# Where the memory steps of a mixing phase stand among its attention heads, the order of its first loads, and four banks for a state update

## What is computed

```python
def step(carry, blk):                       # the matrix memory, branch A
    s = einsum('bhtd,bhsd->bhts', qb, kb) * dmat
    num = einsum('bhts,bhsv->bhtv', s, vb) + w_inter[..., None] * einsum('bhvd,bhtd->bhtv', C, qb)
    h = num / maximum(abs(den), exp(-m_t))[..., None]
    C_new = w_prev[..., None, None] * C + einsum('bhs,bhsv,bhsd->bhvd', w_s, vb, kb)

def sparse_attend(q, k_sel, v_sel, valid):  # branch B
    s = where(valid, einsum('btngd,btknd->btngk', q, k_sel) * B_HD ** -0.5, -inf)
    return einsum('btngk,btknd->btngd', softmax(s), v_sel)

y = sigmoid(a_o) * h * silu(a_z)                       # A, then a projection
merged = sigmoid(g_a) * (ya @ w_a_proj) + sigmoid(g_b) * (yb @ w_b_proj)
x = x + rmsnorm(merged @ w_out, norm_post)             # then a gated layer embedding
```

## Time and profile before

| | us |
|---|---|
| median of 3 runs | 3930.36 (3926.3 to 3934.82) |
| the profiled execution | 3925.36 |
| its span, first to last instruction | 3923.8 |
| mean granted TensorE clock | 0.979 |

### The profile page before, as it was taken

How to read it: one execution, slowest core, us unless ns; L and a number is a source line. 1 busy time by engine, 2 the same in 40 slices (tenths; PEclk the granted TensorE clock), 3 DMA queues, 4 the chain that set the end, 5 groups by cost and what they waited for, 6 DMA issues and landing times. The chain is left out here.

```text
span 3923.8 us, 56232 instructions
## 1 busy us (share of the span) xinstructions
PE 3757.7 (96%) x21590; PEld 2318.8 (59%) x21590; DVE 3012.1 (77%) x4178; ACT 1389.0 (35%) x2337; POOL 1667.8 (43%) x1529
## 2 busy tenths in 40 slices
PE   7899999999999999999999889989997999999999
PEld 4555555564456666666666466766664788854444
DVE  5589999879999999999999477677774677643333
ACT  5411211156244334433332356675552222111111
POOL 0000035549796566665555212234204666642121
PEclk9999999999999999999999899999997999999999
DMA  6312223240112111111211623464244665532111
GB/s 226 93 62 66 69 72 94 102 151 27 57 52 73 66 65 65 58 68 64 71 63 59 149 70 107 124 176 133 86 125 152 186 172 166 172 120 70 40 54 47
DMA packets 303453, 379.99 MB, mean 97 GB/s; under 512 B 74795, under 2 KB 227267, under 8 KB 299990
## 3 DMA queue, kind: packets, MB, share of 16 engines
q1 hardware_dynamic: 262790, 260.48, 22.0%
q0 software_dynamic: 19664, 86.31, 6.1%
q10 hardware_dynamic: 20736, 29.66, 2.4%
HBM read 245.79 MB, written 129.28 MB: 96 GB/s over the span
## 5 line engine op out<-in xcount | busy, mean ns | idle before, releaser
L1315 DVE MAX8 best<-score 128x8 f32<-128x384 f32 (+13 forms) x448 | 639.7, 1428 | 23.3 <-POOL score L1283 8.4
L1317 DVE MATCH_REPLACE8 score<-best,score 128x384 f32<-128x384 f32 (+13 forms) x448 | 631.1, 1409 | 0.0
L1072 PE MATMUL pr<-xnT,w_row 128*128 128x347 f32 (+1 forms) x960 | 298.7, 458 | 0.0
L1813 PE MATMUL mix_slot<-mix_kT,early 128*128 128x512 f32 (+3 forms) x640 | 271.2, 555 | 25.3 <-DMA mix_kT<-qt_scr 10.9
L1826 PE MATMUL mix_po<-mix_ring,mix_v 32*128 32x128 f32 x8704 | 264.9, 275 | 25.2 <-issue 13.3
L1224 POOL TENSOR_TENSOR kT<-kT 128x347 f32<-128x347 f32 (+1 forms) x240 | 193.7, 807 | 211.9 <-ACT kT L1142 204.9
L396 PE MATMUL pg<-xnT,wt 128*128 128x416 f32 x800 | 282.4, 516 | 0.0
L1826 PEld LDWEIGHTS mix_po<-mix_ring,mix_v 32*128 32x128 f32 x8704 | 255.3, 190 | 39.3 <-issue 30.1
L1072 PEld LDWEIGHTS pr<-xnT,w_row 128*128 128x128 f32 x960 | 180.6, 190 | 106.7 <-issue 11.6
L1142 ACT COPY kT<-pr 128x347 f32<-128x347 f32 (+1 forms) x240 | 106.5, 445 | 352.4 <-PE pr L1072 342.2
L396 PEld LDWEIGHTS pg<-xnT,wt 128*128 128x128 f32 x800 | 152.9, 191 | 127.9 <-issue 127.9
(11 more groups left out here) (626 smaller groups left out, 7848.3 us busy)
## 6 DMA issues: line engine op xcount, KB each, us to landing
gt_scr<-kT SPq DMA_DIRECT2D x40, 694.0 KB, 3.3
out_gm<-gt_scr ACTq DMA_DIRECT2D x32, 520.0 KB
gt_scr<-kT SPq DMA_DIRECT2D x20, 692.0 KB, 4.2
wt<-in_w_in SPq DMA_DIRECT2D x22, 512.0 KB, 4.0
w0a<-in_w_in SPq DMA_DIRECT2D x11, 1024.0 KB, 6.6
w_row<-in_w_in SPq DMA_DIRECT2D x10, 1024.0 KB, 6.7
qt_scr<-kT POOLq DMA_DIRECT2D x8, 1040.0 KB, 4.3
early<-ybt_scr SPq DMA_DIRECT2D x4, 2080.0 KB, 9.7
```

Of the source, the lines that this page charges most:

```text
L1072: ins = nc.tensor.matmul(pr[:, b, 0:w], lhs, rhs, start=k == 0, stop=k == 3)
L1315: nc.vector.max(best[:, :], sc).then_inc(top_step, 1)
L1317: nc.vector.match_replace(sc, best[:, :], sc, TAKEN).then_inc(top_step, 1)
L1813: mm(s[:, 0:width], bq[p][:, hh, :], kT[:, lo:lo + width], start=True, stop=True).then_inc(slot_mm, 1)
```

## The change

1. `memory_steps`: the 120 steps of tiles 1 to 15 stand only in the 88 heads with five key tiles or more, spread evenly, so that 32 of those heads take two. Heads 48 to 79 take none. The loads F go two a head.
2. `mixing_events`: X of unit 0 stands ahead of head 6's scores.
3. SP's first loads: the masks of unit 1 ahead of its queries, keys 3 behind them, the decays of tile 1 (L1612) ahead of tile 1's operands and of all values.
4. POOL's first three gathers (six indirect DMAs) stand at head 5, not at the start.
5. Sample memory: all 16 updates stand behind the last turn and take the four banks of `pc` in turn, so update u waits for u - 4; ACT decays the second half too (16 instructions more), and DVE's two products go; `spread_keys` stands behind the last `copy_tile`; POOL takes the weights' differences before the gates.

```diff
@@ def memory_steps
-    for m in range(1, NB):
-        for x, step in enumerate(tile(m)):
-            at[8 * m - 4 + x] = step
+    wide = [n for n in range(4, 8 * NB - 4) if MIX_UNITS[n // GQ][1] >= 4]
+    steps = [(m, x) for m in range(1, NB) for x in range(8)]
+    head = {step: wide[k * len(wide) // len(steps)] for k, step in enumerate(steps)}
+    for m, x in steps:
+        at[head[m, x]] = at.get(head[m, x], []) + tile(m)[x]
     for m in range(2, NB):
+        begin = head[m - 2, 6] + 1 if m > 2 else 4
         for x in range(7):
-            at[8 * m - 12 + x] = at.get(8 * m - 12 + x, []) + [("F", m, x)]
+            at[begin + x // 2] = at.get(begin + x // 2, []) + [("F", m, x)]
@@ def mixing_events
+            if u == 1 and h == 2:
+                events.extend(("X", x) for x in range(GQ))
+                turned = 1
@@ sample memory, POOL: ahead of pool.wait_ge(yb_loaded, 16)
+            pool.wait_ge(wb_loaded, 16 * (KT // 2))
+            for pair in range(COLUMN_PAIRS):
+                lo = 2 * P * pair
+                nc.gpsimd.tensor_tensor(w1[:, 0:4, lo + P:lo + 2 * P], w1[:, 0:4, lo:lo + P], w1[:, 0:4, lo + P:lo + 2 * P], ALU.subtract
+                                        ).then_inc(first_sums, 1)
@@ sample memory, DVE
                 dve.wait_ge(upd_mm, u + 1)
-                if half == 0:
-                    dve.wait_ge(decayed, 4 * (hh + 1))
-                nc.vector.tensor_tensor(C[:, bs, hh, x, :], C[:, bs, hh, x, :], pu[u % 2][:, :].rearrange("p (b e) -> p b e", b=4),
+                dve.wait_ge(decayed, 4 * AH * half + 4 * (hh + 1))
+                nc.vector.tensor_tensor(C[:, bs, hh, x, :], C[:, bs, hh, x, :], pc[:, hh // 2, hh % 2, :].rearrange("p (b e) -> p b e", b=4),
@@ sample memory, ACT
             copy_tile(5, 0)
+            copy_tile(6, 0)
             decay(2)
-            copy_tile(6, 0)
-            decay(3)
             copy_tile(7, 0)
             for x in range(QUARTERS):
                 gate(x)
+            decay(3)
+            act.wait_ge(c_turned, 2 * DB)
+            for hh in range(AH):
+                decay(hh, 1)
@@ sample memory, PE
-                if u < 2:
-                    pe.wait_ge(v.sem, v["qnr"])
-                else:
-                    pe.wait_ge(upd_done, u - 1)
+                if u == 0:
+                    wait_copied(DB - 2)
+                    wait_copied(DB - 1)
+                if u % 8 == 0:
+                    pe.wait_ge(v.sem, v[f"kwz{half}"])
+                if u >= 4:
+                    pe.wait_ge(upd_done, u - 3)
             for b in range(5, DB):
-                update(2 * b - 10)
                 turn(b)
-                update(2 * b - 9)
                 carried(b - 1)
-            update(6)
             carried(DB - 1)
-            for u in range(7, 16):
+            for u in range(16):
                 update(u)
```

More of the change, by code:

```diff
@@ L1679, in _ @@
             load_mask(0)
-            for g in range(1, KEY_GROUPS):
+            for g in (1, 2):
                 load_keys(0, g)
             load_first_values(0)
+            load_mask(1)
             load_queries(1)
-            load_mask(1)
+            load_keys(0, 3)
+            load_decay(sp, 1)
             load_first_memory(1)
@@ L1687, in _ @@
                 load_values(0, g)
-            load_decay(sp, 1)
             load_first_values(1)
@@ L1769, in _ @@
                 nc.gpsimd.memset(pw[x][:, :, :], 0.0).then_inc(s_zero, 1)
-            for j in range(KS - 1):
-                gather(j)
             for e in events:
                 i = e[1]
+                if e == ("S", GQ + 1, 0):
+                    for j in range(KS - 1):
+                        gather(j)
                 if e[0] == "Q" and i + 1 < NB:
@@ L2787, in _ @@
                 nc.gpsimd.tensor_tensor(y, y, zb[x], ALU.mult).then_inc(yb_ready, 1)
[L2788 to L2792, removed]
             pool.wait_ge(yb_ready, QUARTERS)
@@ L2853, in _ @@
             step(nc.vector.reduce_sum(den[:, 0:1], qn[:, :], AX_X), "qnr")
-            copy_tile(4)
+            for b in range(4, DB):
+                copy_tile(b)
+            spread_keys(0)
+            spread_keys(1)
             def update(u):
@@ L2869, in _ @@
             step(nc.vector.reciprocal(den[:, 4:5], den[:, 3:4]), "den3")
[L2870 to L2878, removed]
-            for u in (6, 7):
-                update(u)
             dve.wait_ge(c_used, DB)
@@ L2883, in _ @@
             step(nc.vector.scalar_tensor_tensor(h[:, :], pi[:, 0:DV], den[:, 5:6], intra[:, 0:DV], ALU.mult, ALU.add), "h")
-            for x in range(2):
-                state = C[:, 4:8, :, x, :]
-                ins = nc.vector.tensor_tensor(state, state, wpb[:, :].rearrange("p (h b) -> p b h", b=DB)[:, 4:8, :].unsqueeze(3)
-                                              .to_broadcast([P, 4, AH, P]), ALU.mult).then_inc(decayed, 1)
-            dve.wait_ge(decayed, 4 * AH + 2)
-            for u in range(8, 10):
+            for u in range(8):
                 update(u)
@@ L2894, in _ @@
             step(nc.vector.tensor_scalar(ya[:, 0:P], h[:, 0:P], den[:, 1:2], None, ALU.mult), "ya")
-            for u in range(10, 16):
+            for u in range(8, 16):
                 update(u)
@@ L2912, in gate, with decay @@
                 nc.scalar.activation(zb[x], zb[x], ACT.Sigmoid).then_inc(z_sig, 1)
-            def decay(hh):
-                for b in range(4):
+            def decay(hh, half=0):
+                for b in range(4 * half, 4 * half + 4):
                     at = DB * hh + b
@@ L3008, in update @@
                 half, x, hh = u // 8, u // 4 % 2, u % 4
-                if u < 2:
-                    pe.wait_ge(v.sem, v["qnr"])
-                else:
-                    pe.wait_ge(upd_done, u - 1)
+                if u == 0:
[5 more added lines that the diff above has]
+                    pe.wait_ge(upd_done, u - 3)
                 rows = slice(SR * hh, SR * hh + SR)
-                nc.tensor.matmul(pu[u % 2][:, :], vr[rows, x * P:(x + 1) * P], kwz[rows, 4 * half:4 * half + 4, :].rearrange("p b e -> p (b e)"),
+                nc.tensor.matmul(pc[:, hh // 2, hh % 2, :], vr[rows, x * P:(x + 1) * P], kwz[rows, 4 * half:4 * half + 4, :].rearrange("p b e -> p (b e)"),
                                  start=True, stop=True).then_inc(upd_mm, 1)
```

4 lines of the change are left out of this document (1 added, 3 removed).

## The result

The changed kernel takes 3956.41 us (3950.66 to 3958.81, 4 runs) where the kernel before takes 3930.78 on the same chip: the ratio is 1.0063, with a 95% interval of 1.0046 to 1.0081. The forecast was 3904, 26 us faster; it came out 26 us slower, outside the range.

What follows compares the result with a forecast made beforehand. PE, busy 96% of the span, was taken as the bound, so only its idle or low-clock stretches could give time. Start -9, rest of the mixing about 0, sample memory -17: -26 from 3930.4, so 3904 us, range 3887 to 3923.

Steps and rivals of the forecast that it cites:

- The start, -9: Start of the mixing: earlier decays gain 5.3 us, moved transposes 3.7; together 9 us faster, bounds 3 and 11.
- the 3.7 of the prediction: Start of the mixing: gain from moving unit 0's transposes, at most DVE's 3.66 us of waiting for PE.
- The narrow units, -40 gross: Units 12 to 19: emptied of memory steps, they shrink from 106 us to 65.5.
- Those 34.1 us: PE time of the moved steps in units 12 to 19, said to reappear in the wide units and gain nothing.
- with the share of 80% kept: Units 12 to 19: 52.4 us of remaining full-clock PE work at 80% takes 65.5 us, 13.1 of them waste.
- bounds of 5 to 30: Units 12 to 19: waste between 5 and 30 us, so from a gain of 16 to a loss of 8.
- The wide units, +34 and +8: Wide units: 34.1 us of moved PE work, plus 8 us of extra slot waits for 32 more steps.
- PE sets their pace: Wide units: PE is the bound, busy 237.6 of 246 us and 288.4 of 308.
- The sample memory, -17: Sample memory phase: its new order ends at 3001 instead of 3018.0, gain 17 us, bounds 12 and 20.
- the walk: Sample memory: its new order followed engine by engine (ACT, POOL, DVE) along the timeline to an end at 3001.
- The wide units pay: Rival, wide units: DVE waits at Y, and the slots with it, 12 to 15 us more; 3918 us, chance 0.20.
- The narrow units fall to 1.2 GHz: Rival, units 12 to 19: at half speed throughout they take 105 us; kernel slower, 3945 us, chance 0.05.

Runs made afterwards that it cites:

- e4: The whole change without its memory steps, which stand where they stood before; against the kernel before: 3903.42 us, ratio 0.9938.
- e3: The kernel before with only the new start (first loads, gathers, transposes of unit 0): 3920.69 us, ratio 0.9977.
- e2: The kernel before with only the new sample memory: 3916.63 us, ratio 0.9964.

## Why the steps lose

**Where they stand.** Three other placements.

e5 puts the second of two steps at one head behind that head's exponentials:

```diff
+            events += late.get(n, [])
         events.append(("N", n))
```

> The whole change, but the second of two memory steps at one head comes behind that head's exponentials and the last head's normalisation, not directly behind the first. The first four runs gave the start 8.5 us of gain, the sample memory 12.5, both together 25.7, and the steps alone 45 us of loss. Theory A (the steps stand too close: the second step needs what DVE and ACT make of the first, and four matmuls want three slots): the PE idle time that the steps added in units 1 to 11 and 20 to 30, 22 us, falls by more than half, 3956 - 10 to 20 = 3936 to 3946 us. Theory B (it is the number of steps in those units, that is DVE's and ACT's queues, whatever their distance): within 5 us of the whole change, 3951 to 3961 us.

Measured: 3945.08 us, 11 less than the whole change (ratio to before 1.0037, 1.0023 to 1.0050). In time this is theory A's lower edge. Its mechanism is not borne out: of the 21 us of idle PE that the steps add in units 0 to 11 and 20 to 30 (61.3 beside e4's 39.9), only 4.5 went (56.8), not more than half. Units 20 to 30 took 315 us instead of 328; unit 2 lost 7 us that I can't place.

e7 deals the work out evenly:

```diff
-    steps = [(m, x) for m in range(1, NB) for x in range(8)]
+    steps = [(m, x) for m in range(1, NB) for x in range(14)]
```

> The whole change with the same heads, but the tile's work dealt out in 14 pieces of one matmul group instead of 8 steps of two: two or three groups at a head, never four. Theory A of the run before it (bursts and short distances): at least as good as the split, 3930 to 3946 us. Theory B (number of steps): 3951 to 3961 us. A middle value would say that the slots are a part, and the distance from a step to the next (which stays as short here on the mean) the rest.

Measured: 3942.74 us, ratio 1.0030 (1.0019 to 1.0041). 13.7 less than the whole change, with never four groups at a head: the bursts are a quarter of the loss. Of the idle PE time 7 us went (54.1).

e6 lowers the limit:

```diff
-    wide = [... MIX_UNITS[n // GQ][1] >= 4]
+    wide = [... MIX_UNITS[n // GQ][1] >= 2]
```

> The whole change with the limit at heads of three key tiles or more (104 heads for 120 steps, 16 doubled) instead of five (88 heads, 32 doubled). Dose theory: half the heads are emptied and half are doubled, so half of the 52 us comes back, 3930 us (3924 to 3936). Rival (emptying the narrowest units pays, once the others are not overfull): 3905 us or less. Second rival (what hurts are the emptied narrow units themselves, where PE's clock fell to 0.6 and the load of the values was laid bare): over 3940 us.

Measured: 3934.97 us, ratio 1.0009 (1.0000 to 1.0018). That is 31.5 us more than e4, 60% of the loss, though only 22 of the 56 matmul groups leave the narrow units here. That is inside the dose theory's range, at its upper end, and far from the first rival: with the moderate limit, too, emptying the narrowest units does not pay.

What a doubled head looks like is seen in the timeline of the whole change at head 39 and on, unit 9, where M1, MT and two M2 stand together (start, us, engine, line, out<-in, and in brackets the idle time before it):

```profile
2501.52 0.66 PE L1910 MATMUL mix_slot<-ident,sm_C 128*128 128x128 f32 x4 [0.43 <-DVE mix_mx L2052]
...
2502.26 1.27 ACT L1986 ACTIVATE mix_dmat<-sm_C,par 128x128 f32<-128x128 f32 x4
2502.27 0.67 PE L1926 MATMUL mix_slot<-mix_cT,sm_C 128*128 128x257 f32 x2
...
2503.61 0.69 DVE L2122 TENSOR_TENSOR mix_sd<-mix_slot,mix_dmat 128x512 f32<-128x512 f32 x1 [1.29 <-ACT mix_dmat L1986]
2504.22 0.48 DVE L2130 TENSOR_SCALAR sm_C<-mix_slot,par 128x257 f32<-128x257 f32 x1
...
2504.45 0.67 PE L1926 MATMUL mix_slot<-mix_cT,sm_C 128*128 128x257 f32 x2 [1.50 <-issue]
```

DVE can't empty M1's slot before ACT has made the decays, by the order of the three slots the second M2 needs that slot, and PE stands still for 1.50 us. The profile names no releaser for this wait ("issue"); that it is the slot is read from the order and from the times, DVE's L2122 ending at 2504.30 and PE starting at 2504.45. Such a step is a round trip through three engines.

**What in them costs.** Four pairs of kernels make one engine's share in the steps small, each with the moved steps and without. What is read is the gap within a pair, 53 us with nothing taken away. Their outputs are not the reference's, as their expectations say.

Light Q (e9 and e10):

```diff
-  inter[:, hh, 0:DV], h[:, hh, 0:DV], ACT.Square     den[:, 3, :], ACT.Sqrt
+  inter[:, hh, 0:16], h[:, hh, 0:16], ACT.Square     den[:, 3, :], ACT.Square
```

> The whole change with a light step Q: ACT squares 16 columns of each head instead of 256 and takes the squares' root by a square, so that no table is loaded for it. ACT's block of about 5 us a tile shrinks to about 2. The output is not the reference's. To be read against the next run, the same edit without the change's memory steps; the gap between the two kernels was 52 us with the full Q. Theory A (Q holds ACT's queue, and with the steps closer together DVE's and PE's behind it): the gap falls to 30 us or less, this kernel at 3930 us or below. Theory B (Q is not what the crowding pays for): the gap stays over 42 us.

> The change without its memory steps (3903 us), with the same light Q. The output is not the reference's. PE waited 1.5 to 3 us in some units for DVE's maximum behind that block; I expect 3890 to 3900 us by either theory, and it is the zero for the run before.

Measured: 3931.30 and 3892.74 us. The gap is 38.6: neither theory's number, Q carries about a quarter.

Light DVE part (e11 and e12):

```diff
+  lo = 192 if i else 0
-  inter[:, hh, :]     slot[:, s, 0:DV1]       (M2; M3 and M4 likewise)
+  inter[:, hh, lo:]   slot[:, s, lo:DV1]
```

> The whole change with light work of DVE in the memory steps of tiles 1 to 15: the three kinds of instruction that empty a slot of M2, M3 and M4 (0.48, 0.42 and 0.48 us) handle 65 columns instead of 257, about 0.25 us less for each of 180, 45 us in all. The output is not the reference's. To be read against the next run. Theory C (the steps crowd DVE's queue, so slots come free late): the gap of 52 us falls to 30 us or less. Theory D (the loss is PE's own: its matmul groups don't cancel between narrow and wide units, and its clock falls): the gap stays over 42 us.

> The change without its memory steps (3903 us), with the same light DVE work. The output is not the reference's. DVE is not the bound there, PE is: 3885 to 3900 us by either theory, and it is the zero for the run before.

Measured: 3945.36 and 3901.17 us, a gap of 44.2. In units 0 to 30 it removes 34 us of DVE's work (515.8 to 481.8) and brings 11: theory D's side in the number. D's reason, that the loss is PE's own, is tested by the next pair but one and holds at most in part.

Even, with both reliefs (e13), against both reliefs without the steps (e14):

> The whole change with all three reliefs at once: the 14 pieces dealt evenly, the light Q, and the light DVE part. The output is not the reference's. To be read against the next run, its zero. Theory A (the three are different microseconds): of the gap of 52 us 13.5 + 13 + 8 go, 17 stay (12 to 22). Theory B (they are largely the same waits, each relief lifts the wait that the others would have lifted too): 27 us or more stay.

> The change without its memory steps, with the light Q and the light DVE part. The output is not the reference's. With the light Q alone it was 10.7 us faster, with the light DVE part 2.3: 3890 us by the sum, for either theory the zero of the run before.

Measured: 3919.59 and 3890.36 us, a gap of 29.2: theory B. Apart the reliefs take 14, 14 and 9 us from the gap, together 24; so they lift in part the same time.

Light matmuls (e15 and e16):

```diff
-  mm(s[:, 0:DV1], stands, moves, start=True, stop=True)
+  mm(s[:, lo:DV1], stands, moves[:, lo:], start=True, stop=True)
```

> The whole change with light matmuls in M2, M3 and M4 of tiles 1 to 15: 65 columns instead of 257. The output is not the reference's. A group of this kind took 0.6 us of PE in the wide units; a quarter of the columns leaves at most 0.25. To be read against the next run. Theory C (PE's own work: what the steps add in the wide units is more than what leaves the narrow ones): both shrink, and the gap falls from 52 to 35 to 42 us. Theory D (the gap is waits and the slower products): it stays at 46 us or more.

> The change without its memory steps, with the same light matmuls. The output is not the reference's. 180 groups less by some 0.35 us each, 63 us, if PE is the bound throughout: 3840 us; DVE, which empties the slots in the same time as before, may keep it at 3855. For either theory it is the zero of the run before.

Measured: 3948.00 and 3902.09 us, a gap of 45.9, at the edge of theory D's 46. The surprise is the second: I had expected 3840 to 3855, and taking three quarters of the columns away from 180 matmul groups brought 1.3 us, or 5 when each kernel is counted from the kernel before on its own chip. I had priced a light group too low: 20 of them still took 7.8 us of PE where the full ones took 12.5, which is 0.24 us saved a group and not 0.35. But even the 23 us by which PE's busy time fell in units 0 to 30 (652.1 to 629.4) shortened them by only 3.1. The stretches of e4, then of e16:

```profile
2271.60:2519.90 248.30, 238.11 (x3905) 172.63 (x3905) 179.19 (x470) 156.86 (x242) 51.06 (x56) 1.00 0.35 100
...
2623.40:2917.80 294.40, 274.48 (x4203) 185.86 (x4203) 218.52 (x561) 173.27 (x254) 75.53 (x82) 0.99 0.39 118
```

```profile
2272.60:2516.50 243.90, 226.38 (x3906) 170.50 (x3906) 178.85 (x470) 156.85 (x243) 49.81 (x54) 1.00 0.36 101
...
2621.10:2915.20 294.10, 267.28 (x4203) 189.90 (x4204) 218.00 (x561) 173.29 (x254) 75.74 (x82) 0.97 0.39 118
```

PE is busy 11.7 us less in the first and 7.2 less in the second; the stretches shrink by 4.4 and 0.3. What PE no longer works it waits, or runs at a lower clock (0.97 for 0.99). Its waits for DVE in the first stretch, e4 and then e16:

```profile
PE mix_slot L1923 <- DVE mix_mx L2049: 3.2, 15, 0.4
```

```profile
PE mix_slot L1924 <- DVE mix_mx L2050: 9.5, 23, 0.7
```

The pair's other kernel says the same: in the wide units of the whole change light matmuls took 28 us from PE's busy time and 10.5 from the length. So PE, 96% busy, does not alone set the pace of the wide units. It and DVE hand three slots to and fro, and part of PE's work fills time in which it would otherwise wait. How much the slots matter was measured with one fewer (e18, on e4):

```diff
-SLOTS = 3
+SLOTS = 2
```

> The change without its memory steps (3903 us) with two slots instead of three. Theory A (slots, that is DVE's turn, pace the wide units together with PE): every score piece and memory group then waits for the one two before it, and at 0.5 us or more for some 300 of about 560 slots the kernel is over 100 us slower, above 4000 us. Theory B (PE alone paces them, DVE follows with room to spare): under 30 us slower.

Measured: 3990.26 us, 87 slower than e4, ratio to before 1.0149 (1.0136 to 1.0163): under the 100 us that theory A had set, but near it and far from B. In units 2 to 11 PE then waits so for DVE, with the same work:

```profile
PE mix_slot L1923 <- DVE mix_mx L2049: 13.0, 29, 0.8
```

That is 10 us more than in e4, while the stretch is 31 us longer (279.1): PE's busy time grew by 14 with the same instructions. The clock, 0.99 beside 1.00, accounts for 2.5 of the 14. It seems, then, that a wait for a slot stands partly in the busy time of matmuls, and that the waits of the changed kernel looked harmless for this reason; neither was shown by itself. The run shows that two slots bind, not that three do. A fourth slot, the test in the other direction, was not tried: all eight banks are taken, and the products need four.

**What keeps the narrow units at 86 us.** In every kernel that empties them they last 84 to 91 us, whatever else it does, but for e17 below. PE's costliest group there is the products of probabilities and values; the lines are of the whole change, of e4, whose stretch is 103.5 us long, and of e17 below (xcount | busy us, mean ns | idle before):

```profile
L1834 PE MATMUL mix_po<-mix_ring,mix_v 32*128 32x128 f32 x768 | 33.8, 311 | 11.0 <-DMA mix_v<-r_scr 5.7 <-issue 5.2
```

```profile
L1831 PE MATMUL mix_po<-mix_ring,mix_v 32*128 32x128 f32 x768 | 23.7, 274 | 2.8 <-DMA mix_v<-r_scr 2.8
```

```profile
L1838 PE MATMUL mix_po<-mix_ring,mix_v 32*128 32x128 f32 x768 | 24.6, 281 | 6.4 <-DMA mix_v<-r_scr 6.4
```

The same 768 matmuls take 10 us more once the memory's have left from between them, with 5.2 us of "issue" that e4 has not in these units. One such place in the whole change:

```profile
2583.74 0.51 PE L1834 MATMUL mix_po<-mix_ring,mix_v 32*128 32x128 f32 x3 [0.37 <-issue]
2584.49 0.48 PE L1834 MATMUL mix_po<-mix_ring,mix_v 32*128 32x128 f32 x3 [0.24 <-issue]
2585.21 0.82 PE L1834 MATMUL mix_po<-mix_ring,mix_v 32*128 32x128 f32 x4 [0.23 <-issue]
2586.66 4.67 PE L1834 MATMUL mix_po<-mix_ring,mix_v 32*128 32x128 f32 x77 [0.64 <-issue]
```

For 3 us PE gets three or four matmuls in each 0.7 us. The 77 behind it, in the stretch 2586.30:2591.30, run at a granted clock of 0.50, that is at 1.2 GHz: 61 ns each, for 29 in the wide units. The transfers of 2582 to 2587, by queue (packets, MB, share of the engines):

```profile
q1 hardware_dynamic: 1381, 0.84, 82.8%
q0 software_dynamic: 131, 0.41, 31.0%
q8 instruction: 1, 0.02, 1.6%
```

One packet of instructions went through while the other queues had all sixteen engines busy. e17 takes the gathers away:

```diff
+                    if j >= KS:
+                        pool.dma_start(kvg[j % KS][:, half, 0:32], ...[0:P, 0:32]).then_inc(gathered[j % KS], 16)
+                        continue
                     pool.indirect_dma_start(out=kvg[j % KS][:, half, :], ...
```

> The whole change with light gathers: all but the first four gathers of the sample's keys and values are replaced by plain transfers of 16 KB each, in place of 256 KB. The output is not the reference's. To be read against the whole change, 3956 us, units 12 to 19 at 86.4 us, with PE waiting 5.7 us for the values, 5.2 us in 13 pieces for nothing that the profile shows while the transfers ran at 250 GB/s, and ACT 6.8 us for a store. Theory A (the floor of the narrow units is the traffic): those waits shrink, units 12 to 19 take 70 to 78 us, the kernel 3940 to 3948 us. Theory B (the floor is the chain of one unit through PE, DVE and ACT, with short transfers whose latency, not rate, is waited for): units 12 to 19 stay over 82 us, the kernel over 3950 us.

Measured: 3923.01 us, ratio 0.9977 (0.9968 to 0.9986), 33 less than the whole change and 17 below the range of theory A. Its narrow units:

```profile
2555.50:2625.70 70.20, 57.50 (x956) 42.15 (x955) 42.92 (x176) 45.99 (x122) 20.84 (x37) 0.92 0.47 114
```

70.2 us instead of 86.4: theory A for these units. The issue time before products is gone there (one pause of 2.5 us stands before turned keys instead), the wait for the values is not. The other 15.6 us came in units 20 to 30, which theory A had not named; units 2 to 11, where the same gathers run, kept their 277. e17 has no partner without the steps, so it says what holds the emptied narrow units, not how large the gap would be; and since it changes the number of bytes, the kind of transfer and POOL's time for it (33.4 to 20.8 us) together, which of them starves PE is open.

The Trainium skill (Runtime: NRT & Kernel Launch, Instruction fetch mechanics) says that an engine fetches its next instructions through a DMA queue of its own while it works on the last ones, so that the cost is mostly hidden. If the issue time here is that fetch, which no run isolates, it is hidden in the narrow units of e4, where the memory's matmuls stand among the short ones, and in those of e17, and not in those of the whole change. In units 20 to 30 pauses under this label stand before the products in every kernel looked at: 12.2 us in the whole change, 9.4 in e4, 9.6 in e17, and 9.1 in the kernel before. Long matmuls between the short ones don't prevent them, and the gathers are not their only cause.

**One try at the end of the sample memory** (e8). SP issues four stores of y ahead of the last store of the state, here in the whole change:

```profile
3044.51 5.06 SPq L2771 DMA_DIRECT2D y_scr<-sm_ya  x4
3049.62 0.51 SPq L2764 DMA_DIRECT2D out_o_C_sample<-sm_C  x1
```

DVE was done at 3045.4, so about 4 us of the phase are SP's. e8 gives two of the four to ACT, on e4:

```diff
-            for hh in range(AH):
+            for hh in range(AH // 2):
                 sp.dma_start(d["y"][SEQ:ROWS, ...
...
+            for hh in range(AH // 2, AH):
+                act.dma_start(d["y"][SEQ:ROWS, ...
```

> The change without its memory steps (3903 us), and the sample's four stores of y, which took SP 5.06 us to issue ahead of the last store of the state, dealt to two queues: two by SP, two by ACT. Theory (SP's issuing ends the phase): the last store is issued 2.5 us earlier and the kernel takes 3901 us (2 to 3 us less). Rival (the output phase waits for the stores to land or for its own loads, not for their issue): no change within 1 us, 3903 us.

Measured: 3909.05 us, ratio 0.9945 (0.9932 to 0.9959): neither number, and no gain over e4 clear of the spread (3899 to 3912 us). ACT issued its two in 1.31 us, SP its two in 5.37: it is not their number that holds SP but, as it seems, the three stores of 1 MB ahead of them.

## The prediction, step by step

By the traces the forecast missed by 7 us at the start (-2 for -9), 21 in the narrow units (-19.7 for -40.5), 24 in the wide ones (+66 for +42) and 2 in the sample memory.

- **The start, -9: right by itself, spoilt by the steps.** e3 measured -8.5. In the whole change DVE's wait for tile 1's decays is gone, which answers to the earlier trace rows:

```profile
2236.02 1.26 ACT L1986 ACTIVATE mix_dmat<-sm_C,par 128x128 f32<-128x128 f32 x4
...
2238.40 0.69 DVE L2122 TENSOR_TENSOR mix_sd<-mix_slot,mix_dmat 128x512 f32<-128x512 f32 x1 [0.65 <-issue]
```

  So are the 8.20 us of the earlier trace rows; PE waits 4.43 us behind the moved transposes instead, which keeps 3.8 us of gain, the 3.7 of the prediction:

```profile
2252.69 2.07 PE L1821 MATMUL mix_slot<-mix_kT,early 128*128 128x512 f32 x2 [4.43 <-DVE mix_mx L2052]
...
2262.27 9.21 PE L1834 MATMUL mix_po<-mix_ring,mix_v 32*128 32x128 f32 x320
```

  But the doubled steps at heads 4 and 6 gave 6.1 us back, and the prediction had priced the moved steps only from unit 2 on.
- **The narrow units, -40 gross: half.** Two terms failed. "Those 34.1 us": the stretch lost only 19.4 us of busy PE against e4 (87.50 to 68.06), 10 of the missing 15 because the products took longer. And "with the share of 80% kept": the waste was not a share of the work but had its own causes: the gathers (16 us, e17), the wait for the values (5.7), the clock. It went from 21.6 to 18.3 + 0.12 x 68.1 = 26.5 us, where I had 13.1, and inside the bounds of 5 to 30 that I had given and not weighed.
- **The wide units, +34 and +8: the 34 right, the 8 wrong.** The instructions on `sm_C` added what was forecast. The extra waits were idle time of 9.8 + 10.5 = 20.3 us and about 9 us of low clock (0.99 and 0.97 for 1.00 and 0.99), 29 in all. I had sized them by the 13.2 us of one kind of wait for 88 steps, in proportion. This is the term that failed here, 8 us put down and 29 measured. The step under it, "PE sets their pace" because it is busy for 237.6 of 246 us, does not hold by itself: light matmuls brought 1 to 5 us, one slot fewer cost 87 us. PE's work is part of the price all the same, since the 34 us of moved work did come on top.
- **The sample memory, -17: right, with some luck.** It took 47 us, 15.4 less (12.5 by the kernel's time, e2). DVE's updates stand in rows, and three instructions of one column took 2.2 to 2.3 us beside a POOL that never paused, as the trace before had shown for two of them (the earlier trace rows has one). The lines of DVE and POOL answer to the earlier trace rows:

```profile
L2870 DVE TENSOR_TENSOR sm_C<-sm_C,sm_pc 128x512 f32<-128x512 f32 x16 | 9.9, 682 | 0.8 <-PE sm_pc L3012 0.7
...
L2849 DVE TENSOR_TENSOR sm_kwz<-sm_kw,sm_bm 128x512 f32<-128x512 f32 x2 | 4.1, 2040 | 0.0
...
L2876 DVE TENSOR_TENSOR sm_den<-sm_den,sm_row 128x1 f32<-128x1 f32 x1 | 2.3, 2303 | 0.0
```

```profile
L2789 POOL TENSOR_TENSOR out_w<-out_w 128x512 f32<-128x512 f32 x4 | 5.0, 1278 | 0.0
```

  The updates wait 0.8 us for PE instead of 16.4. The two `sm_kwz` took 2.04 us each; in the kernel before, beside an idle POOL, 0.69. The trace thus agrees with the Trainium skill (SBUF — State Buffer, Who interferes with whom), by which a DVE instruction with two SBUF inputs contends with a GpSimd instruction that reads SBUF. POOL's differences took 1.28 us each; in the kernel before, begun beside DVE's two products of 2048 columns, 2.28. The end of the phase was SP's, not DVE's, which the walk had left out: DVE's last update came 19.6 us earlier in the phase than before, and SP's issuing behind it grew from 2.7 to 7 us. The two errors cancelled in part.
- **The rivals.** "The wide units pay" named the mechanism, slots behind Q and Y, and gave it 12 to 15 us; it was 29 with the clock, and Q is about a quarter of the gap (e9). "The narrow units fall to 1.2 GHz" happened in pieces (clock 0.88). No rival put the two together, and the chance of a slower kernel, 0.06, was for a clock at half speed throughout. A rival that said "the steps are moved from a place where PE has time to one where it has none" would have pointed to it: the narrow units waste 20% of their time, units 2 to 11 waste 3% and units 20 to 30 waste 8%.

What stays open: of the 52 us, 29 remain when steps are even and ACT's and DVE's part in them light. The traces of that pair show 32 us of added PE work (busy time by clock) in units 0 to 11 and 20 to 30 and only 22 freed in the narrow ones. So some 10 us are PE's own work, which does not cancel, and the rest is idle time and clock; which part of it the gathers hold was not tried on the pair.

## What to carry to other kernels

A busy share of 96% does not by itself make an engine the bound when it shares a few buffers with another: make its work small, and see what the time does, before work is moved on that ground. Work in a sparse stretch often fills time that something else sets, so look for what would be left there before taking it out; emptied, the narrow units kept 86 us. Test the parts of a change apart: here two of three were worth 26 us, and the third cost 45 alone and some 52 beside them.

## What was not expected of the hardware

- A run of small matmuls that follow each other at 29 ns can run dry: 13 pauses with 5.2 us in all before the products in units 12 to 19 of the whole change, where e4 and e17 have none, and 9 to 12 us in units 20 to 30 of all four kernels looked at. Behind one of the 13 the granted clock was 0.50 for 5 us.
- Matmuls of 65 columns instead of 257, in 180 groups, took 23 us from PE's busy time and 1 to 5 from the kernel's (3902 and 3903 us).
- ACT's light Q, without two table loads a tile, brought 11 to 13 us even where nothing was moved (e10), though ACT is busy only 440 of the 708 us of units 0 to 30 in e4.
